# Three subtractions of a transformer layer's weight split, moved from VectorE to GpSimd ahead of the first recurrent head

## The reference, cut to what matters

```
h = rmsnorm(x, norm_pre_mix[layer]) * (1.0 + sc_m) + sh_m
proj = h @ w_in[layer]
(hq, hf, hi, hg, aq, ak, av, iq, ik, iw) = jnp.split(proj, split_points, axis=-1)
o_hg = hgrn2_mixer(hq, hf, hi, hg, lb_all[layer], hgrn_out_norm[layer])
o_att = dsa_mixer(aq, ak, av, iq, ik, iw, positions, idx_k_norm_w[layer], idx_k_norm_b[layer])
...
# in dsa_mixer, 8 indexer heads of width 64:
k_idx = layernorm(k_idx, k_norm_w, k_norm_b)
s = jnp.einsum('bqhd,bsd->bqhs', qi, k_idx)
score = jnp.einsum('bqh,bqhs->bqs', wi, jax.nn.relu(s)).astype(jnp.float32)
```

## Time and profile before

| | |
|---|---|
| median of 3 runs | 722.12 us (720.59 to 722.20) |
| the profiled execution | 722.99 us, its span 721.3 us |
| TensorE busy | 698.5 us, 97% of the span |
| VectorE busy | 436.1 us, 60% |
| ScalarE busy | 296.4 us, 41% |
| GpSimd busy | 10.3 us, 1%, 37 instructions |
| granted TensorE clock, mean | 0.993 |

### The profile page before, as it was taken

One profiled execution on the slowest core, in us unless ns is written; L12 is line 12 of the kernel. 1 busy time (PEld: TensorE's weight loads), 2 busy tenths in 40 slices (PEclk: granted clock), 3 DMA queues, 4 the chain that ended last, 5 costly groups with the idle time before them and its releaser, 6 DMA issues.

```text
span 721.3 us, 11007 instructions
## 1 busy us (share of the span) xinstructions
PE 698.5 (97%) x3950; PEld 551.0 (76%) x3950; DVE 436.1 (60%) x815; ACT 296.4 (41%) x471; POOL 10.3 (1%) x37
## 2 busy tenths in 40 slices
PE   4899999999999999999999999999999999999997
PEld 3657577777766787878888888888888788888885
DVE  3866988898898999978733333323332245433444
ACT  6336543535544344536763243342244231211223
POOL 4000000000000000000000000000000000000000
PEclk9899999999999999999999999999999999999999
DMA  8963222232223757467225542345532324223103
GB/s 287 357 176 88 59 60 60 59 117 58 58 61 116 233 177 245 163 233 201 63 60 145 145 133 78 93 132 145 159 102 88 97 79 146 87 89 113 61 0 118
DMA packets 96155, 89.10 MB, mean 124 GB/s; under 512 B 3110, under 2 KB 85114, under 8 KB 96124
## 3 DMA queue, kind: packets, MB, share of 16 engines
q1 hardware_dynamic: 96124, 88.70, 40.8%
HBM read 86.59 MB, written 2.10 MB: 123 GB/s over the span
## 4 chain that ended last, share of the span: by engine, by line
PE 64%; DVE 2%; issue 0%; DVEq 0%; ACT 0%
PE ps L1335 36%; PE ps L1356 17%; PE ps L1374 6%; PE ps L1641 1%; PE ps L1621 1%; PE ps L1395 1%; PE ps L1753 1%; PE ps L1757 1%; PE ps L1754 1%; PE ps L1515 0%; PE ps L1509 0%; PE ps L1634 0%; DVE w_lo L816 0%; DVE act L917 0%; DVE act L1142 0%
## 5 line engine op out<-in xcount | busy, mean ns | idle before, releaser
L1335 PE MATMUL ps<-h_hi,w_hi 128*128 128x512 f32 x560 | 226.5, 405 | 0.0
L1335 PE MATMUL ps<-h_hi,w_lo 128*128 128x512 f32 x560 | 218.7, 390 | 0.0
L1335 PE MATMUL ps<-h_lo,w_hi 128*128 128x512 f32 x560 | 218.3, 390 | 0.0
L816 DVE TENSOR_TENSOR w_lo<-w_raw,w_hi 128x1024 fp32r<-128x1024 f32 (+1 forms) x109 | 129.3, 1187 | 98.3 <-ACT w_hi L458 97.8
L458 ACT ACTIVATE w_hi<-w_raw 128x1024 fp32r<-128x1024 f32 (+1 forms) x109 | 111.4, 1028 | 109.7 <-PE ps L1356 86.3
L1335 PEld LDWEIGHTS ps<-h_hi,w_hi 128*128 128x128 f32 x560 | 105.2, 188 | 26.5 <-issue 5.0
L1335 PEld LDWEIGHTS ps<-h_hi,w_lo 128*128 128x128 f32 x560 | 105.1, 188 | 22.6
L1335 PEld LDWEIGHTS ps<-h_lo,w_hi 128*128 128x128 f32 x560 | 105.3, 188 | 21.1 <-issue 1.0
L1356 PE MATMUL ps<-w_hi,h_hi 128*128 128x512 f32 x176 | 70.1, 398 | 0.8 <-DVE mix L1207 0.8
L1356 PE MATMUL ps<-w_hi,h_lo 128*128 128x512 f32 x176 | 68.6, 390 | 0.0
L1356 PE MATMUL ps<-w_lo,h_hi 128*128 128x512 f32 x176 | 68.5, 389 | 0.0
(11 more groups left out here) (246 smaller groups left out, 785.1 us busy)
## 6 DMA issues: line engine op xcount, KB each, us to landing
w_raw<-in_w_ffn_in SPq DMA_DIRECT2D x44, 512.0 KB, 6.0
w_raw<-in_w_in SPq DMA_DIRECT2D x28, 512.0 KB, 3.9
w_raw<-in_w_ffn_out SPq DMA_DIRECT2D x22, 512.0 KB, 3.5
adaw<-in_w_ada SPq DMA_DIRECT2D x12, 512.0 KB, 4.0
act<-in_w_ada SPq DMA_DIRECT2D x12, 512.0 KB, 8.9
adaw<-in_w_ada SPq DMA_DIRECT2D x6, 1024.0 KB, 5.2
act<-in_w_ada SPq DMA_DIRECT2D x6, 1024.0 KB, 5.1
res<-in_x SPq DMA_DIRECT2D x8, 512.0 KB, 5.2
```

Of the source, the lines that this page charges most:

```text
L816: V.tensor_tensor(w_lo[slot][:, 0:n], w_raw[slot][:, 0:n], w_hi[slot][:, 0:n].bitcast(f32), ALU.subtract).then_inc(lo_ok, 1)
L1335: last = mm(ps[bank][0:rows, :], a, b, start=(k == 0 and n == 0), stop=(k == KT - 1 and n == 2))
```

## The change

Three of the subtractions leave VectorE's order and go to GpSimd: those of groups `G_HG + 2`, `G_HG + 3` and `G_HG + 4`. GpSimd waits for the rounded part (`hi_ok`) and for the count of the group before (`lo_ok`), so that the count still rises in order. VectorE gets one wait of its own in head 0, so that its next subtraction comes after GpSimd's third.

```
@@ gpsimd
             pool.memset(at_diag, 0.0).then_inc(at_zero, 1)
+
+            def split_lo(g, slot):
+
+                pool.wait_ge(hi_ok, g + 1)
+                pool.wait_ge(lo_ok, g)
+                pool.tensor_tensor(w_lo[slot][:, :], w_raw[slot][:, :], w_hi[slot][:, :].bitcast(f32),
+                                   ALU.subtract).then_inc(lo_ok, 1)
+
+            split_lo(G_HG + 2, 2)
+            split_lo(G_HG + 3, 3)
+            split_lo(G_HG + 4, 0)
             pool.wait_ge(att_out, ATT_HEADS)
@@ vector
             rotate_iq(1, 2)
-            split_lo(G_HG + 2, 2)
             rotate_iq(2, 3)
             ve.wait_ge(wt_ok, 1)
             score_four(0)
             rotate_iq(3, 4)
             score_four(4)
-            split_lo(G_HG + 3, 3)
             for n in range(8, 24, 4):
                 score_four(n)
             ve.wait_ge(causal_ok, TT - 1)
-            split_lo(G_HG + 4, 0)
@@ vector, in hg_body
                     elif st in (1, 3, 6, 8):
                         at, slot = {1: (5, 1), 3: (6, 2), 6: (7, 3), 8: (8, 0)}[st]
+                        if isinstance(h, int) and h == 0 and st == 1:
+                            ve.wait_ge(lo_ok, G_HG + 5)
                         split_lo(h * 4 + (G_HG + at), slot)
```

## The result

The changed kernel takes 724.49 us in the median of 7 runs (723.80 to 726.09), the kernel before 722.12 (720.59 to 722.50). The ratio is 1.0031, with a 95% interval of 1.0016 to 1.0045. The profiled execution took 724.19 us, its span is 722.5. Measured again later the ratio was 1.0039 (1.0026 to 1.0053). So the change costs 2 to 3 us, about 0.3 to 0.4%.

The account below looks back on a forecast made before the run. TensorE, busy for 97% of the span, was taken to bound the kernel. It would stand 3.4 us and regain 1.5, so 1.9 us more than the 722.12 median: 724.0 us, range 720.4 to 726.2.

Parts of the forecast that it names:

- VectorE in TensorE's way only among the scores, 1.5 us to be had: Indexer's score blocks: TensorE gets back 0.48 us in the fourth and 1.03 us in the fifth, 1.5 us together.
- 2.2 us for a GpSimd subtraction: GpSimd: one subtraction of 1024 columns takes 2.2 us, estimated from copies in the trace.
- my bounds of 0.96 and 2.7 us: One GpSimd subtraction: at least a 1024-column fill, 0.96 us; at most two operands read one behind the other, 2.7 us.
- The 0.1 us that I put aside: GpSimd's 192-column copy of 0.339 us: some 0.1 us taken not to grow with size, for the upper bound.
- The engines can't read at once when both read two operands: Key's and queries 1's rotation: VectorE and GpSimd hold each other for whole instructions, VectorE 3.5 us late.
- TensorE stands 3.4 us and gets 1.5 back, +1.9 us: Score blocks: TensorE stands 3.4 us in the first and regains 1.5 us later, 1.9 us more in sum.
- 4.7 us that I had named as a sign: TensorE's first score block would stretch from 1.25 to some 4.7 us if the forecast was right.
- The third subtraction for nothing: Start of the recurrence: GpSimd's third holds L1079 to L1084, ending near 102.1 before TensorE asks at 102.3; costed at nothing.
- The rival of no collision: The engines read side by side or GpSimd gives way: gain of 1.5 us, 720.6 us; chance 0.24.
- faster: Outcome of the changed kernel being faster beyond the 0.3%, 2.2 us, that can't be told from none; chance 0.06.
- The rival of the falling clock: TensorE's clock also falls around the first-block stall, losing 1.7 us more: +3.6 us, 725.7 us; chance 0.19.
- full clock: The forecast itself: collision among the rotations with TensorE's clock not falling, 1.9 us more, 724.0 us; chance 0.36.

Follow-up runs that it names:

- the fills: Changed kernel with each of GpSimd's three subtractions replaced by two zero fills of the same tile, which read nothing; ratio 0.9995 (0.9980 to 1.0010).
- the copies: Changed kernel with GpSimd copying the raw weights instead of subtracting, so reading one operand; ratio 0.9993 (0.9978 to 1.0008).
- the early kernels: Kernel before, with slots 2 and 3 rounded earlier and both subtracted early, on VectorE (ratio 0.9994, again 1.0001) or on GpSimd (0.9991).
- two on top: Kernel before, all subtractions still on VectorE, plus two like subtractions on GpSimd into an idle buffer; ratio 1.0046 (1.0029 to 1.0063).
- the first two on GpSimd: Changed kernel with the third subtraction back on VectorE behind the scores; ratio 1.0050 (1.0033 to 1.0067).

## Why the prediction was right

It forecast 724.0 us, in a range of 720.4 to 726.2. It came out at 724.49. The mechanism was the one forecast, two reading engines of which one holds the other. That the total came so near is in part luck: both terms were about 0.2 us too small and have opposite signs, and the later measurement of the same kernel came to 725.95 beside a kernel before of 722.50.

Point by point:

*VectorE in TensorE's way only among the scores, 1.5 us to be had.* Right, and a little more. The return was 1.71 us: 0.49 in the fourth block and 1.03 in the fifth, as worked out, and 0.17 in the third, which takes 1.99 us now against 2.16. There I had counted no loss. The fills, the copies and the early kernels gave 1.64 to 1.70 us.

*2.2 us for a GpSimd subtraction.* Nearly: 2.39 us beside an idle VectorE, and 2.48 where a VectorE instruction was still running at its start. The estimate of 2.25 us from the Trainium skill's GPSIMD Engine Reference, section 3.1, was as near. By either, my bounds of 0.96 and 2.7 us were wide. The 0.1 us that I put aside in the upper one stood in no row; the two copies leave 0.17.

*The engines can't read at once when both read two operands.* Shown for the first part of it. Three kernels whose GpSimd reads two operands there have a first part longer by 3.63 or 3.64 us (the changed kernel's second profile by 3.94, with the start of a spell in it), the one that only writes has none beyond its spell, and the same reads placed in VectorE's pauses have none. The delay of queries 1 was 3.64 us by VectorE's own timeline (L1038 to the end of L1011 is 10.36 us, L1027 to the end of L1000 was 6.72), and I had taken 3.5. The order was as worked through: 1.45 us on the first product (forecast 1.55), 2.20 us on the second. Only "both read two operands" was too narrow, as the copies showed.

What ran here agrees with the Trainium skill. Its page SBUF — State Buffer, section "Who interferes with whom", says that a VectorE instruction with two SBUF inputs collides with a GpSimd instruction that reads SBUF, and not with one that only writes it. It also says that copies and tensor_scalar instructions can enter a mode in which they collide with GpSimd. An instruction with two SBUF inputs was held by a GpSimd instruction that reads, for 2.20 us (2.88 instead of 0.68) of the 2.39 that a subtraction takes. It wasn't held by one that only writes (0.66 and 0.68 us beside the fills). One with a single SBUF input and one from PSUM was not held (L1037 0.69 us beside a subtraction). And tensor_scalar instructions from SBUF to SBUF were held even by fills (1.19 and 1.14 us). That these were in that mode, no trace shows.

*TensorE stands 3.4 us and gets 1.5 back, +1.9 us.* Right in sum: +3.63 - 1.71 = +1.92. The place of the stall was not as I had it. TensorE does not stand only inside the first block. The key is late too, so it stands 1.45 us ahead of the block and 1.97 us inside it (the changed kernel's second profile). So the block itself never came near the 4.7 us that I had named as a sign; it takes 3.28 us (72.89 to 76.17), and 3.68 in the second profile with 0.31 of low clock in it. A reader with that sign alone would have called the forecast wrong.

*The third subtraction for nothing.* Right in the sum, wrong in the margin. I held L1079 to L1084 until 100.4 and came to an end of L1084 near 102.1 for a TensorE that asks at 102.3. On the chip the small copy ahead of them (L1084 in the new numbers) was held. The last result came at 101.60, which is 102.44 on the time scale of the profile before (0.84 us added), and TensorE had already begun at 101.18, which is 102.02 there. It could, because its very first products wait only for L1089, done at 101.00, and those right behind them for the last result. The first 64 records took 0.93 us instead of 0.76, so 0.17 us may have gone there.

*The rival of no collision* was refuted, and with it faster. *The rival of the falling clock* was not refuted. It came in two of the four profiles whose TensorE stalled there (0.57 and 0.58 from 76 to 80 us) and in none of the other eight. I had put 0.19 beside 0.36 for full clock, that is one in three. Of the other two, the kernel with two on top had one at 88 us. With such a spell the changed kernel's second stretch came to +3.56, this rival's +3.6, and its median that time, +3.45, is nearer to this rival than to the forecast. I take these spells to be what puts the changed kernel's medians at +2.4 and +3.5 us, over the +1.9 of a profile without one. The granted clocks of all executions fit that weakly: their mean is 0.9908 in the 25 executions of kernels with the whole stall and 0.9917 in the 74 of the kernel before taken beside the experiments, which on 722 us is 0.6 us of work, but each mean is uncertain by 0.0004. So the excess over +1.9 us is argued, not shown, and so is it that a stall raises the chance of a spell.

## What to carry to other kernels

Work on an idle engine isn't free when its reads hold the busy one: a subtraction of 1.13 us that is moved from VectorE to GpSimd held VectorE for 1.45 to 2.2 us, because it took 2.4 us there and ran beside two-operand instructions. Look first for the pauses of the engine that is to be relieved. Here both subtractions fitted into them, on either engine, once ScalarE's roundings came earlier, and the stretch became 1.7 us shorter instead of 1.9 longer. That this makes the whole program faster than before is not shown: in two of the three profiles of the early kernels some 1.5 us were lost again to a longer spell of low clock behind the stretch. And where a change of 0.2% is at stake, compare the stretch in two profiles: here spells of low clock moved single executions by 1.7 us each, and the medians of the early kernels could not show what their stretches did.

## What the runs showed of the hardware that was not expected

A copy of 2 columns and a tensor_scalar of 4 columns, SBUF to SBUF, took 2.33 and 2.25 us instead of 0.17 beside a GpSimd subtraction. In the changed kernel's second profile it was L1087, a tensor_scalar of 512 columns, with 2.67 us instead of 0.55. I had reckoned with two-operand instructions only. It works the other way too: the first of the fills began at 65.57 under a tensor_scalar that ended at 65.88, and took 1.21 us instead of 0.96.

A spell of low clock can be hidden. In the changed kernel's first profile one of 3.4 us lay at 63 to 67 us (0.58 in that window), but TensorE would have waited for VectorE anyway, and the first part came to 15.70 us. The kernels with the first two on GpSimd and with two on top had one at the same place, and 15.71 us each. The changed kernel's second profile had none there, and its 16.01 us less the 0.31 that a later spell took from the block's second half (1.01 instead of 0.70) are 15.70 again. In the kernel with the fills nothing hid it, and it cost 1.5 us (13.55 against 12.05).
